# MLA output: b powers of four tiles by VectorE inside six heads, eleven between weight tiles, none by POOL; one rotation table per weight tile

## The reference

```python
o = softmax(q_pos @ keys_lat | q_free @ keys_ctx) @ ckv      # 16 heads
v = einsum('bnhc,chv->bnhv', o, w_uv).reshape(b, n, 2048)
y = (v * silu(gate)) @ w_out                                 # 2048 -> 1024: the MLA output
x = layernorm(alpha * x + gt * y)
```

```python
lam_bar = exp(lam * dt)
b_bar = ((lam_bar - 1) / lam)[..., None] * bmat
powers = exp(lam * dt * arange(1, 129))
```

## Time and profile before

| | us |
|---|---|
| median of 3 runs | 2136.4 (2133.89 to 2142.81) |
| profiled execution, its own time | 2128.27 |
| its span in the trace | 2126.5 |
| PE busy | 1980.4 (93%) |
| DVE busy | 1493.4 (70%) |
| ACT busy | 907.8 (43%) |
| POOL busy | 673.2 (32%) |

### The profile page before, as it was taken

The page is one execution under the profiler, slowest core; times in us unless marked ns, Lnnn a source line. Parts: engine busy times, 40 slices in busy tenths (PEclk is TensorE's granted clock), DMA queues, the critical chain, the costliest instruction groups (busy, mean ns, idle before and its releaser), DMA issues.

```text
span 2126.5 us, 42816 instructions
## 1 busy us (share of the span) xinstructions
PE 1980.4 (93%) x17574; PEld 1615.5 (76%) x17574; DVE 1493.4 (70%) x2045; ACT 907.8 (43%) x1532; POOL 673.2 (32%) x485
## 2 busy tenths in 40 slices
PE   7999898899998999888998979999999999999997
PEld 6787777777885555555578867888877799999885
DVE  3366555468985677888866336888994798898834
ACT  3335443343324444333463447555543544343423
POOL 2553211230017999899400111111121111111000
PEclk9999999999999999999999989999999999999998
DMA  9221343432452122232137654999985323333421
GB/s 366 86 91 60 123 159 124 164 134 75 159 193 71 65 90 85 97 119 102 72 109 261 227 218 126 311 297 307 317 273 174 131 98 111 108 100 108 140 90 40
DMA packets 127507, 317.90 MB, mean 149 GB/s; under 512 B 12128, under 2 KB 59104, under 8 KB 120912
## 3 DMA queue, kind: packets, MB, share of 16 engines
q1 hardware_dynamic: 112032, 243.14, 34.3%
q0 software_dynamic: 10672, 53.14, 6.9%
q10 hardware_dynamic: 4608, 18.88, 2.4%
HBM read 238.69 MB, written 76.41 MB: 148 GB/s over the span
## 4 chain that ended last, share of the span: by engine, by line
PE 72%; DVE 12%; DMA 6%; ACT 5%; issue 4%; POOL 1%; SPq 0%; ACTq 0%; DVEq 0%; POOLq 0%
PE psum L521 15%; PE psum L3732 13%; PE psum L2014 7%; PE psum L3156 6%; DMA made_table<-table_made 3%; PE psum L2617 3%; PE psum L1193 3%; PE psum L2580 2%; PE psum L2668 2%; PE psum L2592 2%; PE psum L3326 2%; PE psum L334 2%; PE psum L3276 1%; DVE early L2715 1%; PE psum L3385 1%
## 5 line engine op out<-in xcount | busy, mean ns | idle before, releaser
L3156 PE MATMUL psum<-h,u_w 128*128 128x256 f32 (+1 forms) x768 | 158.2, 352 | 8.1 <-DVE h L3086 5.0
L3689 POOL TENSOR_TENSOR ring<-ring 128x1024 f32<-128x1024 f32 x16 | 54.1, 3383 | 316.3 <-DVE xT L3683 316.3
L510 POOL TENSOR_TENSOR u_w<-ring,u_w 128x512 fp32r<-128x512 f32 x42 | 54.0, 1286 | 273.9 <-ACT u_w L498 257.7
L521 PE MATMUL psum<-h_split,in_w 128*128 128x512 f32 x600 | 139.1, 392 | 1.5 <-POOL in_w L510 1.5
L3156 PEld LDWEIGHTS psum<-h,u_w 128*128 128x128 f32 x768 | 119.2, 192 | 27.7 <-issue 12.9
L521 PEld LDWEIGHTS psum<-h_split,in_w 128*128 128x128 f32 x600 | 111.9, 188 | 27.2 <-ACT prev L857 2.1
L510 POOL TENSOR_TENSOR in_w<-ring,in_w 128x512 fp32r<-128x512 f32 x50 | 77.4, 1549 | 79.2 <-ACT in_w L498 77.0
L2326 POOL TENSOR_TENSOR early<-early,power 128x1024 f32<-128x1024 f32 x44 | 99.7, 2266 | 4.6 <-DMA early<-made_b_bar 1.9
L2014 PE MATMUL psum<-x_high,ring_split 128*128 128x512 f32 x272 | 101.1, 394 | 0.0
L2617 PE MATMUL psum<-area,ckv_tm 128*128 128x512 f32 (+1 forms) x256 | 100.4, 545 | 0.0
L503 DVE TENSOR_TENSOR w_split<-ring,w_split 128x512 fp32r<-128x512 f32 x54 | 40.4, 748 | 84.1 <-ACT w_split L498 83.9
(11 more groups left out here) (527 smaller groups left out, 5403.8 us busy)
## 6 DMA issues: line engine op xcount, KB each, us to landing
ring<-in_s_glu SPq DMA_DIRECT2D x64, 512.0 KB, 3.3
ring<-in_w_mod SPq DMA_DIRECT2D x48, 512.0 KB, 5.7
c_pow<-made_c_pow SPq DMA_DIRECT2D x32, 576.0 KB, 5.1
ring<-in_s_in SPq DMA_DIRECT2D x32, 512.0 KB, 6.9
b_pow<-made_b_pow SPq DMA_DIRECT2D x15, 1024.0 KB, 10.4
ring<-in_w_in SPq DMA_DIRECT2D x25, 512.0 KB, 3.3
made_table<-table_made ACTq DMA_DIRECT2D x16, 768.0 KB, 3.5
table<-made_table SPq DMA_DIRECT2D x32, 384.0 KB, 6.2
```

Of the source, the lines that this page charges most:

```text
L510: nc.gpsimd.tensor_tensor(rounded(buffer(u, 1)), source(u), buffer(u, 0), ALU.subtract).then_inc(pool_done, 1)
L521: ins = nc.tensor.matmul(out, rounded(buffer(u, w)[:, ks]), values(x, k), start=(first and k == 0 and n == 0), stop=(last and k == UNIT_K ...
L3156: ins = nc.tensor.matmul(o, rounded(u_w[:, u % 4, w, kk * P:(kk + 1) * P]), h3_part(x, k)[:, a:a + size], start=(k == 0 and n == 0), stop= ...
L3689: nc.gpsimd.tensor_tensor(left_plain(i, "S3"), left_plain(i, "A11"), left_plain(i, "S3"), ALU.subtract).then_inc(pool_done, 1)
```

## The change

POOL makes no b powers any more. VectorE makes those of tiles 0 to 3 inside heads 9 to 14, four steps of one operation each per head, and those of tiles 4 to 14, 66 steps, inside its loop of the MLA output, five per weight tile. POOL keeps the stores and loads of each tile. ScalarE makes one table per weight tile (two behind the first) instead of four per three. In VectorE's loop the residual of tile m - 1 moves behind the first rest and two steps of pass m. SP waits for b powers of tile 3, not 10, before the reload of the residual stream, and the wait for heads and tables with the loads behind it moves from weight tile 15 of the MLA output to the second tile of the S5 input weights, three entries later in SP's list.

```diff
-POOL_B_POW = 11
+EARLY_B_POW = 4
+B_POW_HEAD = 9
+B_POW_A_HEAD = 4
...
         def b_pow_early_pool(pool):
...
-            for m in range(POOL_B_POW):
-                pool.wait_ge(b_bar_loaded[m % 2], 16 * (m // 2 + 1))
-                if m >= 2:
-                    pool.wait_ge(b_pow_stored[m % 2], 16 * (m // 2))
-                for o, a, b, op in b_pow_parts(m, b_pow_made[m % 2], b_bar_read[m % 2], pool_tmp):
-                    nc.gpsimd.tensor_tensor(o, a, b, op).then_inc(pool_done, 1)
-                    pool.wait_ge(pool_done, pool_count.up("s5", "b_pow", m))
+            for m in range(EARLY_B_POW):
+                pool.wait_ge(*at("s5", "b_pow", m))
                 pool.dma_start(io["b_pow"][m], b_pow_made[m % 2]).then_inc(b_pow_stored[m % 2], 16)
...
         def b_pow_pool(pool):
...
-                if m >= POOL_B_POW + 2:
-                    ln2.add_pool(pool, m - POOL_B_POW - 1)
-            for k in range(KE - 1 - POOL_B_POW - 1, KD - 1):
+                while added < KD - 2 and 2 * (m - EARLY_B_POW) >= 3 * (added + 1) + 2:
+                    added += 1
+                    ln2.add_pool(pool, added)
+            for k in range(added + 1, KD - 1):
                 ln2.add_pool(pool, k)
...
+        def b_pow_dve(dve, m, step, out, b_bar, part):
+
+            if step == 0:
+                dve.wait_ge(b_bar_loaded[m % 2], 16 * (m // 2 + 1))
+                if m >= 2:
+                    dve.wait_ge(b_pow_stored[m % 2], 16 * (m // 2))
+            o, a, b, op = b_pow_parts(m, out[m % 2], b_bar[m % 2], part)[step]
+            nc.vector.tensor_tensor(o, a, b, op).then_inc(dve_done, 1)
+            dve.wait_ge(dve_done, dve_count.up("s5", "b_pow", m))
+
+        def b_pow_early_dve(dve, a, b):
+
+            for n in range(a, b):
+                if 0 <= n < STEPS_B_POW * EARLY_B_POW:
+                    b_pow_dve(dve, n // STEPS_B_POW, n % STEPS_B_POW, b_pow_made, b_bar_read, pool_tmp)
...
+            early = B_POW_A_HEAD * (h - B_POW_HEAD)
...
+                if pair == 1:
+                    b_pow_early_dve(dve, early + 1, early + 2)
                 normalize_dve(dve, n + 2 * pair + 1)
                 if pair == 0 and late_here:
                     c_pow_steps_dve(dve, late, late + 1)
+                if pair == 0:
+                    b_pow_early_dve(dve, early, early + 1)
+                if pair == 2:
+                    b_pow_early_dve(dve, early + 2, early + 4)
...
-                while made < min(KE, 4 * (i + 1) // 3):
+                while made < min(KE, i + 2):
                     table_act(act, made)
...
+            for m in range(KD):
+                first = 2 * m * B_POW_A_SLOT
+                mla_out_w_dve(dve, 2 * m + 2)
+                b_pow_beside_dve(dve, first, first + 2)
+                if m > 0:
+                    residual(m - 1)
+                b_pow_beside_dve(dve, first + 2, first + B_POW_A_SLOT)
+                mla_out_w_dve(dve, 2 * m + 3)
+                if m == 0:
+                    dve.wait_ge(x_back, 2 * 16)
+                v.tensor_scalar(h2[:, m, :], h2[:, m, :], ALPHA_2, None, ALU.mult).then_inc(dve_done, 1)
+                dve.wait_ge(dve_done, dve_count.up())
+                b_pow_beside_dve(dve, first + B_POW_A_SLOT, first + 2 * B_POW_A_SLOT)
+            residual(KD - 1)
...
-                if n == slot_of[("mla_out", 15)]:
+                if n == slot_of[("s5_in", 1)]:
                     for who in ("pe", "act", "dve", "pool"):
                         sp.wait_ge(*at("end", "heads", who))
                     for made in table_stored:
                         sp.wait_ge(made, 16 * KE // 2)
```

More of the change, by code:

```diff
@@ L2320, in b_pow_early_pool @@
                 pool.dma_start(b_bar_read[m % 2], io["b_bar"][m]).then_inc(b_bar_loaded[m % 2], 16)
-            for m in range(POOL_B_POW):
-                pool.wait_ge(b_bar_loaded[m % 2], 16 * (m // 2 + 1))
-                if m >= 2:
-                    pool.wait_ge(b_pow_stored[m % 2], 16 * (m // 2))
-                for o, a, b, op in b_pow_parts(m, b_pow_made[m % 2], b_bar_read[m % 2], pool_tmp):
-                    nc.gpsimd.tensor_tensor(o, a, b, op).then_inc(pool_done, 1)
-                    pool.wait_ge(pool_done, pool_count.up("s5", "b_pow", m))
+            for m in range(EARLY_B_POW):
+                pool.wait_ge(*at("s5", "b_pow", m))
                 pool.dma_start(io["b_pow"][m], b_pow_made[m % 2]).then_inc(b_pow_stored[m % 2], 16)
-                if m + 2 < POOL_B_POW:
+                if m + 2 < EARLY_B_POW:
                     pool.dma_start(b_bar_read[m % 2], io["b_bar"][m + 2]).then_inc(b_bar_loaded[m % 2], 16)
@@ L2334, in b_pow_pool @@
             pool_count.up("s5", "split_zero")
-            for m in range(POOL_B_POW, POOL_B_POW + 2):
+            added = 0
+            for m in range(EARLY_B_POW, EARLY_B_POW + 2):
                 pool.dma_start(b_bar_in[m % 2], io["b_bar"][m]).then_inc(b_bar_loaded[m % 2], 16)
-            for m in range(POOL_B_POW, KE - 1):
+            for m in range(EARLY_B_POW, KE - 1):
                 pool.wait_ge(*at("s5", "b_pow", m))
@@ L2390, in b_pow_last_dve, with b_pow_beside_dve @@
                 tt(im, im, part, ALU.add)
-        def b_pow_dve(dve, m):
-            dve.wait_ge(b_bar_loaded[m % 2], 16 * (m // 2 + 1))
-            dve.wait_ge(b_pow_stored[m % 2], 16 * (m // 2))
-            for o, a, b, op in b_pow_parts(m, b_pow_out[m % 2], b_bar_in[m % 2], dve_tmp[:, 0:TPD * STEP * GS]):
-                nc.vector.tensor_tensor(o, a, b, op).then_inc(dve_done, 1)
-                dve.wait_ge(dve_done, dve_count.up("s5", "b_pow", m))
+        STEPS_B_POW = 6
+        def b_pow_dve(dve, m, step, out, b_bar, part):
[10 more added lines that the diff above has]
+                    b_pow_dve(dve, n // STEPS_B_POW, n % STEPS_B_POW, b_pow_made, b_bar_read, pool_tmp)
+        def b_pow_beside_dve(dve, a, b):
+            for n in range(a, min(b, STEPS_B_POW * B_POW_BESIDE)):
+                b_pow_dve(dve, EARLY_B_POW + n // STEPS_B_POW, n % STEPS_B_POW, b_pow_out, b_bar_in, dve_tmp[:, 0:TPD * STEP * GS])
         def set_table_act(act, function):
@@ L2972, in mla_out_act @@
                 mla_out_w_act(act, i + 2)
-                while made < min(KE, 4 * (i + 1) // 3):
+                while made < min(KE, i + 2):
                     table_act(act, made)
                     made += 1
-        B_POW_BESIDE = KE - 1 - POOL_B_POW
+        B_POW_BESIDE = KE - 1 - EARLY_B_POW
+        B_POW_A_SLOT = -(-STEPS_B_POW * B_POW_BESIDE // (2 * KD - 1))
         def mla_out_dve(dve):
@@ L2983, in mla_out_dve, with residual @@
             h3_gain_dve(dve)
-            for m in range(KD):
-                mla_out_w_dve(dve, 2 * m + 2)
-                if m < B_POW_BESIDE:
-                    b_pow_dve(dve, POOL_B_POW + m)
-                if m == 0:
-                    dve.wait_ge(x_back, 2 * 16)
-                v.tensor_scalar(h2[:, m, :], h2[:, m, :], ALPHA_2, None, ALU.mult).then_inc(dve_done, 1)
-                dve.wait_ge(dve_done, dve_count.up())
-                mla_out_w_dve(dve, 2 * m + 3)
+            def residual(m):
                 dve.wait_ge(*at("mla_out", m))
@@ L4021, in _ @@
                 if n == slot_of[("head", HEADS - 1)] + RING:
-                    sp.wait_ge(*at("s5", "b_pow", POOL_B_POW - 1))
+                    sp.wait_ge(*at("s5", "b_pow", EARLY_B_POW - 1))
                     for i in range(2):
-                        sp.wait_ge(b_pow_stored[i], 16 * ((POOL_B_POW + 1 - i) // 2))
+                        sp.wait_ge(b_pow_stored[i], 16 * ((EARLY_B_POW + 1 - i) // 2))
                     sp.dma_start(h2[:, :, CTX:TC], io["x_kept"]).then_inc(x_back, 16)
                     sp.dma_start(h2[:, :, 0:CTX], io["ctxT"]).then_inc(x_back, 16)
-                if n == slot_of[("mla_out", 15)]:
+                if n == slot_of[("s5_in", 1)]:
                     for who in ("pe", "act", "dve", "pool"):
```

## The result

| | before | after |
|---|---|---|
| median of the timed runs, us | 2135.14 (2132.59 to 2142.81) | 2108.96 (2106.93 to 2115.76) |
| profiled execution, us | 2128.27 | 2106.93 |
| its span, us | 2126.5 | 2105.2 |

The ratio of the times is 0.9877, with a 95% interval from 0.9843 to 0.9911: 26.2 us faster by the medians. The forecast was 2108, in a range from 2092 to 2126. A later group of runs gave the changed kernel a median of 2109.17 and a ratio of 0.9874.

A forecast was written before the change was run, and what follows sets the result against it. Bounds: POOL's b powers delaying VectorE, hence TensorE, in heads 8 to 13, and ScalarE's table chain in the MLA output. Heads 26.2 - 3 = 23.2, plus 5, gives 28.2 us; 2136.4 - 28.2 = 2108 us, range 2092 to 2126.

The forecast's parts named there:

- The three parts: Heads: removing POOL's arithmetic returns 26.2 us, VectorE's 24 steps cost 3, POOL's remaining stores and loads cost nothing.
- two gaps: Head's end: VectorE's slack of 1.14 us before the query projection and 0.92 before the next scores, against two steps' 2.52.
- The rival of the full length: Heads: the two steps at a head's end cost their full length, 15 us, total 2120 us; chance 0.09.
- that of the stores: Heads: POOL's 1 MB stores, which remain, cause the stretch, not its arithmetic; gain 0 to 5 us, about 2130; chance 0.06.
- The walk: MLA output: VectorE's passes followed one by one in before-trace times, last output tile ending at 1246.3; gain 5 us.
- Four sums: MLA output: POOL's sums of the residuals each lengthen a VectorE pass by 1.9 us, in four passes before pass 6.
- a wait of 0.4 for tile 5: MLA output: ScalarE rounds weight tile 5 at 1140.5, so VectorE waits 0.4 us.
- The residual rule: MLA output: TensorE's output tile m + 1 needs pass m's first rest, two steps and residual, 5.0 us.
- moving SP's loads of the next stage costs nothing: End of MLA output: loads three entries later are free, the last table being made near 1230 and stored before the end.
- TensorE-bound: MLA output: POOL's sums cost VectorE little, so TensorE sets the pace; stage gains 12.7 us, total 2100 us; chance 0.14.
- Stores as the bound: MLA output: b power stores landing late hold VectorE, making the kernel slower, 2161 us at 16 us landings; chance 0.05.
- the other reading of the prediction: MLA output: two-input VectorE operations lock only against GpSimd operations reading SBUF, so POOL's queue isn't starved; sum stays 28.

The follow-up runs named there:

- run 6: Changed kernel with the powers of tiles 0 to 3 (24 operations) made by POOL again, not by VectorE in the heads; 2112.9 us, ratio 0.9923.
- run 1: Changed kernel with VectorE's 24 b power steps in heads 9 to 14 shrunk to one-column memsets; 2101.34 us, ratio 0.9835.
- run 12: The changed kernel again, unedited, on one chip with three other runs; 2109.17 us, ratio 0.9874.
- run 2: Changed kernel with one of VectorE's two steps at a head's end moved behind the fourth normalization; 2104.3 us, ratio 0.9842.
- run 5: Kernel before with each of POOL's 66 b power operations replaced by a memset, stores and loads kept; 2111.47 us in one execution.
- run 4: Kernel before with only the change's table schedule and SP's wait moved as there; POOL keeps its b powers; 2130.1 us, ratio 0.9977.
- run 3: Changed kernel with POOL's sums of the residuals, from the third on, cut to one column; 2106.47 us, ratio 0.9856.
- run 9: Kernel before with the change's tables and moved SP wait, plus one more table ahead from the twelfth loop entry; 2131.86 us, ratio 0.9978.

## Why the prediction was right

**The number.** The forecast gain was 28.2 us; the medians give 26.2 and the stages 27.0 (23.5 + 4.4 - 0.9). That the forecast of 2108 lies within 1 us of the measured 2108.96 is partly luck: its base of 2136.4 was 1.3 us above the median with a fourth run, 2135.14.

**Heads, 23.2 forecast, 23.5 measured.** The three parts hold singly. Removing POOL's arithmetic gives heads of 26.63 (26.7 expected); run 6 gets the same price from a third of the dose. VectorE's steps cost 0.52 per head where 0.5 was worked out from two gaps, and run 1 returns 3.2 us without them. One thing was not foreseen: head 7 takes 28.08 instead of 26.72 in this trace, with POOL's angles beside c power steps. In run 12, the same program, it is 26.73, so it changes from one execution to the next; that the two engines met at another phase is my reading and not shown. The rival of the full length (15 us) is refuted by runs 1 and 2, that of the stores by run 5; the stores stay in the changed kernel's heads and cost nothing visible there.

**Output stage, 5 forecast, 4.4 measured.** The walk held nearly pass by pass: with the 18.3 us by which this trace's stage starts earlier taken off, pass 1 was to begin at 1114.1 and did at 1114.7, pass 6 at 1206.1 and 1206.4, the end was to be at 1228.0 and came at 1228.6. Inside it two errors cancel, which is luck. Four sums were charged 1.9 us each and a wait of 0.4 for tile 5, 8.0 together; a sum costs a step 1.5 (2.75 instead of 1.23; POOL's own operation stretches to 2.88), only three of them met a step before pass 6, and tile 5 was on time, so this was 4.6. But the roundings of weight tiles 7 and 8, assumed on time, were late behind table stores and made VectorE wait 1.89 and 1.39 us, 3.3 together. The residual rule, that TensorE's next tile waits for the start of VectorE's pass, shows as 8.8 us with the residual as releaser.

**Wrong in its own steps.** The text expected no wait of ScalarE for table stores beyond the first three; there are 14, of 56.7 us. That waiting was already there (56.6 us before, and 58.9 in run 4, whose stage is 12 us shorter) and mostly costs nothing, for ScalarE has one table per 8 us to make: I had mistaken the wait for the price, where the price was two tables in a row. And "moving SP's loads of the next stage costs nothing" is right at this stage's length only: 0.8 us here, 5.8 when the stage is 12 us shorter.

**The rivals.** TensorE-bound (12.7 us of stage, so one of 130.4) is near what run 3 shows when sums are taken out (132.9), not what happened. Stores as the bound: no row of it; the Trainium skill's rule ("SBUF — State Buffer", section "SBUF: two separate sides") that a DMA of GpSimd's queue starves beside a 2-port operation of VectorE would have shown as a later landing, and a median of 6.1 us against 5.7 isn't the 10.7 worked out for it. The b power steps are two-input operations, and the landings agree with the other reading of the prediction, that these don't starve the queue.

**Not settled.** The medians of runs 1 and 2 fell by more than their stages explain. The share that two-input operations have in the price of the heads rests on run 5 alone, one execution with shorter POOL operations. And the size of the stretch in the heads is not one number: heads 8 to 13 took 186.4 us in the trace before, 189.9 in run 4's and 196.5 in run 9's, with the same work in them (granted clock 0.97, 0.98 and 0.93).

## What to carry to other kernels

Price a collision by the operation: find the same instruction with and without the neighbour, multiply, and then check whether the engine that is held has slack. Before you shorten a stage, look at what stands in the queues of SP, POOL and VectorE for the start of the next one, because an in-order queue that waits for a late store, or is still busy with late work, gives the gain back (6 to 8 us of 6 to 12 here, and a second such wait under the first). A long total wait on an engine is no price unless something downstream waits for it.

## What the hardware showed that I had not expected

A memset on POOL left VectorE's two-input operations untouched (1359 ns for 128x1152) and stretched its one-input multiply to 1695 ns; arithmetic on POOL stretched both (3311 and 2063). Not every operation is hit: of VectorE's two such multiplies in a head, the earlier one (into `ctxT`) kept its 1359 ns beside the arithmetic too. In this kernel constant fills were much cheaper neighbours than arithmetic: the six heads took 165.0 us beside memsets, 186.4 beside the arithmetic and 159.7 in run 1, with neither. And two-input operations on both engines share the loss: beside a VectorE that never pauses, POOL's sum took 2.88 us instead of 1.88, and VectorE's step 2.75 instead of 1.23.

Behind the output stage TensorE does short products with pauses, and the granted clock is lower: over the 32 us of run 4 from the last product to the first S5 product it is 0.66, over the 24 us of the kernel before 0.70. The 64 products on the c powers took 1.96 us at a granted clock of 0.50 (the level of 1.2 GHz) after the wait of 5.76, and 1.16 us at 1.00 (2.4 GHz) in the kernel before, where they follow the last product at once. The stretches, kernel before and run 4:

```profile
1251.23:1275.48 24.25, 12.61 (x138) 6.48 (x139) 14.65 (x19) 14.96 (x20) 6.92 (x6) 0.70 0.74 271
```

```profile
1239.64:1271.72 32.08, 13.76 (x139) 7.68 (x139) 14.67 (x19) 15.48 (x22) 6.91 (x6) 0.66 0.71 263
```

With a wait of 5.8 us the stretch is 7.8 longer. TensorE's busy time in it is 1.2 us longer (13.76 instead of 12.61), 0.8 of that in these products; what made the rest isn't shown.
